# Strassen-like feed-forward groups of a hybrid encoder step: new queue orders on ScalarE and VectorE, one product's adds on VectorE, and a last group in plain tiles

## What is computed

```
h = h + W_out [ shortconv_group(RMSNorm(h)) ; retention_group(RMSNorm(h)) ]
f = square(relu(RMSNorm(h) @ w_up)) @ w_down      # 1024 -> 4096 -> 1024
y = RMSNorm(h + f) * norm_final_w
```

## Time and profile before

| | us |
|---|---|
| median of 3 runs (lowest, highest) | 1333.43 (1333.05, 1334.88) |
| the profiled execution, its device time | 1337.05 |
| its span in the profile | 1335.3 |
| TensorE busy | 1248.4 (93%) |
| VectorE busy | 809.3 (61%) |
| ScalarE busy | 561.0 (42%) |
| GpSimd busy | 402.0 (30%) |

### The profile page before, as it was taken

The page is one execution under the profiler, slowest core; times in us unless marked ns, Lnnn a source line. Parts: engine busy times, 40 slices in busy tenths (PEclk is TensorE's granted clock), DMA queues, the critical chain, the costliest instruction groups (busy, mean ns, idle before and its releaser), DMA issues.

```text
span 1335.3 us, 20703 instructions
## 1 busy us (share of the span) xinstructions
PE 1248.4 (93%) x6780; PEld 1135.2 (85%) x6780; DVE 809.3 (61%) x1322; ACT 561.0 (42%) x1113; POOL 402.0 (30%) x288
## 2 busy tenths in 40 slices
PE   8999999999999899799999999999999999999983
PEld 6999999999998788688888888798788888888882
DVE  7544544553555334577667658757767667666757
ACT  6232132232223222544544554554554454454446
POOL 0000000000000000275366356357346437536532
PEclk9999999999999899899999999999999999999996
DMA  6111111111114400310110210210210111011003
GB/s 219 46 42 44 43 35 50 42 29 48 41 49 150 119 1 28 91 54 19 55 55 16 63 55 8 63 55 8 63 55 19 51 55 44 26 55 55 1 16 134
DMA packets 88338, 70.18 MB, mean 53 GB/s; under 512 B 9440, under 2 KB 73056, under 8 KB 88304
## 3 DMA queue, kind: packets, MB, share of 16 engines
q1 hardware_dynamic: 88304, 69.73, 17.2%
HBM read 64.73 MB, written 4.99 MB: 52 GB/s over the span
## 4 chain that ended last, share of the span: by engine, by line
PE 52%; issue 19%; POOL 17%; DVE 6%; DMA 3%; ACT 2%; POOLq 1%; SPq 0%; DVEq 0%; ACTq 0%
PE ps L1304 16%; PE ps L1306 15%; PE ps L1305 15%; POOL h L1292 11%; POOL do_raw L1278 2%; POOL do_raw L1275 2%; DVE do_lo L1159 2%; POOL do_raw L1280 2%; POOL fo_raw L1285 1%; DMA normw<-in_norm_ffn_w 1%; DVE ws_lo L1137 1%; ACT fr L759 1%; DVE hw L1204 1%; DVE h L1181 1%; ACT fr L757 1%
## 5 line engine op out<-in xcount | busy, mean ns | idle before, releaser
L1292 POOL TENSOR_TENSOR h<-tmp,h 128x512 f32<-128x512 f32 x184 | 254.5, 1420 | 120.2 <-ACT tmp L774 120.2
L1304 PE MATMUL ps<-mid_hi,ws_hi 128*128 128x368 f32 (+1 forms) x768 | 254.8, 332 | 35.5 <-DVE ws_lo L1137 34.3
L1306 PE MATMUL ps<-mid_hi,ws_lo 128*128 128x368 f32 (+1 forms) x768 | 252.9, 329 | 0.0
L1305 PE MATMUL ps<-mid_lo,ws_hi 128*128 128x368 f32 (+1 forms) x768 | 252.7, 329 | 0.0
L1304 PE MATMUL ps<-hn_hi,ws_hi 128*128 128x368 f32 (+1 forms) x648 | 219.7, 339 | 1.5 <-DVE hn_lo L910 1.5
L1305 PE MATMUL ps<-hn_lo,ws_hi 128*128 128x368 f32 (+1 forms) x648 | 213.2, 329 | 0.0
L1306 PE MATMUL ps<-hn_hi,ws_lo 128*128 128x368 f32 (+1 forms) x648 | 213.0, 329 | 0.0
L1304 PE MATMUL ps<-do_hi,fo_hi 128*128 128x512 f32 x448 | 179.8, 401 | 25.5 <-DVE h L1181 17.1
L1275 POOL TENSOR_TENSOR do_raw<-dr 128x512 f32<-128x512 f32 x16 | 26.4, 1647 | 535.8 <-DMA dr<-in_w_down 535.3
L774 ACT ACTIVATE tmp<-ps 128x512 f32<-128x512 f32 x184 | 110.2, 599 | 171.5 <-PE ps L1306 153.3
L1304 PEld LDWEIGHTS ps<-mid_hi,ws_hi 128*128 128x128 f32 x768 | 145.6, 190 | 40.8 <-issue 26.8
(11 more groups left out here) (181 smaller groups left out, 1816.8 us busy)
## 6 DMA issues: line engine op xcount, KB each, us to landing
raw<-in_w_up SPq DMA_DIRECT2D x64, 256.0 KB, 3.2
...
```

What stands on the lines that cost most here:

```text
L1292: pool.tensor_tensor(h_part(p, q), tmp(k, last), h_part(p, q), ALU.add).then_inc(pool_add, 1)
L1304: pe.matmul(out, a_hi, b_hi, start=start, stop=False, skip_group_check=again)
L1305: pe.matmul(out, a_hi, b_lo, start=False, stop=False, skip_group_check=again)
L1306: return pe.matmul(out, a_lo, b_hi, start=False, stop=stop, skip_group_check=again)
```

## The change

Five edits, all in the feed-forward part:

1. ScalarE's queue in groups 0 to 14: the `d_hi` copies are spread among the Relu and Square, the a = 1 weight split stands third instead of eighth, `S1` ahead of `S2`, the copies for GpSimd stand among the last `f_hi`. VectorE's queue: only one `d_low` (B11) ahead of the two weight splits, the other six between them and the `f_low`; `f12` ahead of S1; S1's sum, then `add(P1, 0)`, then S2.
2. The four adds of product P4 go from ScalarE and GpSimd to VectorE: VectorE has 20 adds a group, GpSimd 8, ScalarE 8 copies.
3. The sample's two banks are added with two VectorE adds of 128 partitions for four of 64, into `h` rows of which the upper 64 are set to zero once (a memset of 64 x 1024 in the output projection); the last group folds the upper rows into the lower with two ScalarE copies and two adds.
4. The loads of `w_down` still wait for all seven `d_low` of the group before, whose last (T3) is now later in the group.
5. Group 15 has no Winograd form. Behind `up`, TensorE goes tile by tile over 128 tokens, in the order 4, 5, 6, 7, sample, 0, 1, 2, 3: the eight blocks' plain product, 12 matmuls of 512 columns a tile (8 for the sample). VectorE adds `h` in place in PSUM, ScalarE squares from PSUM, takes the root, and scales the upper half of the tile into `hw`, which GpSimd multiplies by `normw` for the first seven tiles; VectorE does the lower half.

```diff
-ORDER_LAST = [(p, q) for p in (P1, P2) for q in range(QUADS)] \
...
-DVE_ADDS = [(P1, 0), (P1, 1), (P1, 2), (P1, 3), (P2, 0), (P2, 1), (P2, 2), (P2, 3), (P5, 0), (P5, 1), (P7, 0), (P7, 1),
-            (P5, 2), (P7, 2), (P7, 3), (P5, 3)]
+DVE_ADDS = [(P1, 0), (P1, 1), (P2, 0), (P1, 2), (P1, 3), (P2, 1), (P2, 2), (P2, 3), (P5, 0), (P5, 1), (P7, 0), (P7, 1),
+            (P7, 2), (P7, 3), (P5, 2), (P5, 3), (P4, 3), (P4, 0), (P4, 1), (P4, 2)]
-POOL_ADDS = [(p, q) for p in (P6, P4, P3) for q in range(QUADS)]
+COPIES = [(P6, 0), (P6, 1), (P6, 2), (P6, 3), (P3, 0), (P3, 1), (P3, 2), (P3, 3)]
-FIN = [0, 1, 4, 5, 8, 2, 3, 6, 7]
+FIN = [4, 5, 6, 7, 8, 0, 1, 2, 3]
+FIN_PAIRS = [(6, 7), (0, 1), (2, 3), (4, 5)]
+FIN_POOL = 7
...
+            def final_root(p):
...
+                act.wait_ge(fin_add, 2 * p + 1)
+                if p:
+                    act.wait_ge(fin_step, 3 * p)
+                act.activation(tmp0[0:n, :], fin_source(p, 0), ACT.Square, accum_out=fin[0:n, t, 0:1]).then_inc(fin_step, 1)
...
+                act.wait_ge(fin_add, 2 * p + 2)
+                act.activation(tmp0[0:n, :], fin_source(p, 1), ACT.Square, accum_out=fin[0:n, t, 1:2]).then_inc(fin_step, 1)
...
+                act.activation(fin[0:n, t, 3:4], fin[0:n, t, 1:2], ACT.Sqrt, scale=1.0 / D, bias=fin[0:n, t, 2:3]).then_inc(fin_sd, 1)
...
+            def final_scale(p):
...
+                if p >= 2:
+                    act.wait_ge(y_out[p % 2], 32 * (p // 2))
+                act.activation(hw[0:n, p % 2, 512:1024], fin_source(p, 1), ACT.Copy, scale=fin[0:n, t, 0:1]).then_inc(y_scaled, 1)
...
+                for p in range(TILES):
+                    final_root(p)
+                    if 1 <= p <= FIN_POOL:
+                        final_scale(p - 1)
...
+                    dve.memset(h[SAMPLE:P, TILES - 1, :], 0.0)
...
+                for p in range(TILES):
+                    final_add(g, p)
+                    if p >= 1:
+                        final_norm(p - 1)
+                final_norm(TILES - 1)
...
+            for p in range(FIN_POOL):
+                n = rows(FIN[p])
+                pool.wait_ge(y_scaled, p + 1)
+                pool.tensor_tensor(hw[0:n, p % 2, 512:1024], hw[0:n, p % 2, 512:1024], normw[0:n, 512:1024],
+                                   ALU.mult).then_inc(y_pool, 1)
...
+            def final_tile(g, p, t):
...
+                elif p >= 4:
+                    pe.wait_ge(y_low, p - 3)
+                    pe.wait_ge(y_scaled, p - 3)
+                parts = [("f1", "f2")] if t == TILES - 1 else [("A11", "A12") if t < 4 else ("A21", "A22")]
```

More of the change, by code:

```diff
@@ L824, in group @@
                 f_hi(g, "A11")
[L825 to L827 removed]
+                relu(g, 0, 2)
+                square(g, 0, 2)
+                up_split(g, "up", 1)
+                f_hi(g, "A21")
                 f_hi(g, "f1")
[L829 to L833 removed]
@@ L1262, in _ @@
-            with dve.Fori(0, GROUPS - 1) as g:
-                group(g, False)
-            group(GROUPS - 1, True)
+                    dve.wait_ge(fold_in, nh + 1)
+                    dve.wait_ge(samp_add, 2 * g)
+                    dve.tensor_tensor(h[0:SAMPLE, TILES - 1, sl], [tmp0, tmp1][nh][0:SAMPLE, :], h[0:SAMPLE, TILES - 1, sl],
+                                      ALU.add).then_inc(fold_done, 1)
+                f_low(g, "A11", F_HI_END)
+                f_low(g, "A21", F_HI_END)
@@ L1577, in sample, with group @@
                                              do_lo[:, D_OF[name], :], start=x == 0, stop=x == 1)
                     last.then_inc(prod_done, 1)
-            def group(g, first, last_group):
+            def group(g, first):
                 up(g, first)
-                for step in ORDER_LAST if last_group else ORDER:
-                    if step == "sample":
-                        sample(g, last_group)
-                    else:
-                        product(g, *step, first, last_group)
@@ L1588, in _ @@
-            group(0, True, False)
-            with pe.Fori(1, GROUPS - 1) as g:
-                group(g, False, False)
-            group(GROUPS - 1, False, True)
+                for p in range(OPS):
+                    for q in range(QUADS):
+                        product(g, p, q, first)
+                sample(g)
+            def final_tile(g, p, t):
+                if p == 0:
+                    pe.wait_ge(samp_add, 2 * g)
+                elif p == 1:
+                    pe.wait_ge(relu_done, 6 * g + 2)
+                elif p == 2:
+                    pe.wait_ge(relu_done, 6 * g + 6)
+                elif p >= 4:
+                    pe.wait_ge(y_low, p - 3)
+                    pe.wait_ge(y_scaled, p - 3)
+                parts = [("f1", "f2")] if t == TILES - 1 else [("A11", "A12") if t < 4 else ("A21", "A22")]
+                for nh in range(2):
+                    out = ps[FIN_PAIRS[p % 4][nh]][:, :]
+                    for k, name in enumerate(parts[0]):
+                        if nh == 0:
+                            pe.wait_ge(f_ready, NF_PARTS * g + F_LO_END.index(name) + 2)
+                        block_b = [["B11", "B12"], ["B21", "B22"]][k][nh]
+                        pe.wait_ge(d_ready, ND_PARTS * g + D_END.index(block_b) + 1)
+                        b = d_slot(block_b)
+                        if t == TILES - 1:
+                            last = passes_sample(out, sf[:, k, :], do_hi[:, b, :], do_lo[:, b, :], start=k == 0, stop=k == 1)
+                        else:
+                            a, at = f_slot(name), t % 4 * P
+                            last = passes(out, fo_hi[:, a, at:at + P], fo_lo[:, a, at:at + P], do_hi[:, b, :], do_lo[:, b, :],
+                                          start=k == 0, stop=k == 1)
+                    last.then_inc(prod_done, 1)
@@ L1594 @@
+            group(0, True)
+            with pe.Fori(1, G_LAST) as g:
+                group(g, False)
+            up(G_LAST, False)
+            for p, t in enumerate(FIN):
+                final_tile(G_LAST, p, t)
 _INS = ["x_prompt", "x_sample", "state_conv", "state_ret", "meta_tokens", "norm_mix_w", "w_in", "conv_w", "ret_gn_w",
```

539 lines of the change are left out of this document (296 added, 243 removed).

## The result

The changed kernel takes 1261.35 us, the median of 4 runs (1259.95 to 1264.14), against 1334.16 us (1333.05 to 1335.44) for the kernel before, measured beside it. The ratio is 0.9457, with a 95% interval of 0.9435 to 0.9478. The gain is 72.8 us; 69.0 were forecast. The profiled execution took 1264.14 us, of which 1262.2 are its span.

A forecast was written before the change was run, and what follows sets the result against it. TensorE sets the pace, others matter where it waits. Repeated groups 47.5, group 0 5.9 and last group 15.6 sum to 69.0 us off the median 1333.43: 1264.4, own range 1256 to 1273, 8 in 10 from 1255 to 1280.

The forecast's parts named there:

- The wait for `ws_lo` in `up`: TensorE's wait in the middle of a = 1, for VectorE's weight subtract, goes with 3 us to spare: -1.77 us a group.
- two causes: For ws_lo: GpSimd's four adds fewer end T1 some 5.1 us sooner, and ws_hi stands behind T1 alone on ScalarE.
- The waits in P4: Two TensorE waits in P4 for VectorE's adds of P7 go, as those adds move ahead of P5's: -1.25 us a group.
- The wait for A12's low part: TensorE's wait at P2's first matmul shrinks from 0.81 to 0.44 us; bounds: nothing stays, or all 0.81.
- The order of S4 and A12's low part: Rival: GpSimd's S4 takes the ports first, if 0.06 us sooner than reckoned; +19 us, 1284; chance 0.08.
- The mis-sized term: The repeated group's period becomes 45.24 us, 3.39 less; over 14 groups -47.5 us.
- Group 0: TensorE's wait for ws_lo there shortens by 4.3 us; with 1.6 from the P waits, -5.9 us.
- the 4.3: In group 0, how much sooner TensorE goes on after its ws_lo wait, taken from 4.2 to 5.5 us.
- The last group: Group 15 with plain tiles takes 57.0 us for 72.60, a gain of 15.6 (from 9.8 to 18.1).
- the rival of the clock: The last group's tiles run at the lower clock level: +8 to +20 us, 1272 to 1284; chance 0.08.
- The slower rival: VectorE's ten subtracts behind the weight split meet GpSimd operations; all ten give 9.6 us a group and 1408; chance 0.03.
- the other three rivals: S4 first at the ports (0.08), lower clock in the last group (0.08), waits returning elsewhere, 1312 or so (0.03).

The follow-up runs named there:

- the late T1: The changed kernel, but P4's four adds are back with ScalarE's copies and GpSimd: 1262.47 us.
- both undone: The changed kernel, but with 12 adds a group on GpSimd and the a = 1 weight split as ScalarE's eighth operation: 1275.67 us.
- the run with the subtractions first: The changed kernel, but VectorE makes A22's low part, the next group's ws_lo and S4's low part ahead of P5's and P7's adds: 1301.48 us.
- the run with four buffers: The changed kernel, but with four buffers for the finished rows in place of two: 1263.64 us.

## Why the prediction was right, step by step

**What bounds it.** Right: the idle time of TensorE was the gain, and its busy time stayed.

**The wait for `ws_lo` in `up`.** Right that it goes, and with room: `ws_lo` is done 7.5 us into a group where the prediction had 8.6 (1028.1 - 1019.55): it runs for 0.69, not 1.9, since it starts 0.14 ahead of GpSimd's T4. With the late T1 it takes 1.85 and is done at 9.8, still in time. The prediction named two causes and did not say whether one would do. The runs show that either is enough and that a third had a share. With both undone 0.80 of the 1.77 came back (0.88 in the group's length); the rest hangs on the six low parts that stood ahead of the split on VectorE. The prediction saw those only as a danger in their new place.

**The waits in P4.** Right in place and mechanism, shown by the run with the subtractions first. (Of P5's adds only the last two went behind P7's, not all four as the prediction reads.) VectorE's four new adds cost nothing on the path, as was said: the group is as long with them on GpSimd (44.984) as on VectorE (44.997). Moving P4's adds brought nothing that the new queue orders alone don't bring. That the prediction did not say.

**The wait for A12's low part.** Right: 0.36 of 0.81 stays, forecast 0.44; operations stand 0.60 apart on VectorE, not 0.63. The order of S4 and A12's low part, on which a rival rested, held with 0.16 us to spare for the reckoned 0.06, in each of the 15 groups.

**The mis-sized term: 3.39 a group.** It was 3.64, so 3.4 us are missing in 14 groups. Of the 0.25, 0.08 is the term above. 0.10 is the step behind `ws_lo`'s wait, which the prediction left out: in the earlier trace rows the wait ends at 1033.23 and the next matmul starts at 1033.49, 0.26 for 0.16, while for P2 and P4 it did count the slower step behind the wait. The last 0.07 is spread over steps too small to name.

**Group 0.** Forecast 5.9, measured 5.0; two profiles of the same code for group 0 lie 0.9 apart (56.15 and 55.21). The step that was off is when `w_down` is in, which the prediction took from the trace before. Counted from the group's first matmul, GpSimd starts T1 at 16.3 us (536.43) where it was 15.1 before; in the profile with 55.21 it is 15.9. The length of `ws_lo`, 1.79 beside GpSimd's T2, is near the upper bound of 1.9, and that bound was what the 4.3 went by. So TensorE went on 3.2 us sooner, outside the 4.2 to 5.5 that was given.

```profile
536.43 1.26 POOL L1366 TENSOR_TENSOR do_raw<-dr 128x512 f32<-128x512 f32 x1 [535.98 <-DMA dr<-in_w_down]
538.91 1.79 DVE L1195 TENSOR_TENSOR ws_lo<-raw,ws_hi 128x512 fp32r<-128x512 f32 x1 [5.46 <-ACT ws_hi L748]
```

**The last group.** Forecast 57.0, measured 55.99. TensorE's last matmul starts at 1253.39, 47.2 us in, where 47.5 was the forecast for its end, with steps of 0.227 throughout: the rival of the clock did not happen. (Its price had a slip: the twelve matmuls behind 1276.77 cost some 0.13 more each, not 0.07.) ScalarE did keep pace: roots come 2.72 us apart where it follows TensorE, of which it waits 0.22 for VectorE's add, so it needs 2.5 a tile for the reckoned 2.7. The first root starts at 27.0 for 25.9, the last ends at 50.5 for 49.6 to 50.2. Without a wait on write-outs the end would then be at 54.85 for 54.5; the 2.5 us for these waits were too much: 1.14 at the end, and by the run with four buffers 1.12 is all they cost. Of the 16.6 us won, by starts in both traces, 3.9 lie in `up` (27.6 to 23.7; a wait and a stretch at the lower clock go), 5.9 in the products, though they are 104 matmuls for 92, and 6.8 behind the last matmul (15.6 to 8.8). No run takes the plain tiles apart from the rest, so the share of each edit in this group isn't shown.

**The slower rival.** Its block of ten subtractions ran with one of them stretched, where one or two were reckoned (from 950.52 on two `do_lo` take 2.38 for 1.28), and the ranges of the other three rivals were not touched.

**What was put at nothing, and the sum.** The folds and the later loads of `w_down` cost nothing: `up` of the last group takes 23.7 for the forecast 23.9, and no gap in a repeated group answers to the loads. The memset stands in the part ahead of group 0, whose end scatters by 5.8 us, so its price can't be read. The terms missed by +3.4, -0.9 and +1.0, and 0.6 came from that scatter: only group 0 helped to bring the sum nearer. The forecast's own range of 1256 to 1273 is narrower than its three bounds give when they are added, some 1254 to 1276; the measured 1261 lies well inside either.
